# Two transformer blocks in one kernel: query tiles ahead of the gated units, and a first tile in three interleaved passes

## The chip, the cores and the metric

One core of a Trainium2 chip runs the whole program. The metric is the device time of one execution in microseconds (us). TensorE (PE) does the matrix products, VectorE (DVE), ScalarE (ACT) and GpSimd (POOL) do the elementwise work, and SyncE (SP) issues nearly all DMAs. Each engine runs its own instruction list in order and waits on semaphores for the others.

## The reference, cut to what matters

The kernel computes a hybrid layer (sparse attention beside a gated convolution, then cross attention, then a gated feed-forward net) and after it a recurrent layer, for 512 tokens of width 1024. The change lies in the first part of the first layer:

```
h = rmsnorm(x, norm_mix_g);  proj = h @ w_in
q, k, v, qi, ki, wi, glu = split(proj)              # q 512 wide, glu 2*512 wide
q, k, qi, ki = partial_rope(...)                    # tables from the positions
# attention: index scores relu(qi.ki)*wi, top 128 keys per query, 8 heads, 4 query blocks of 128
u  = glu_a * sigmoid(glu_g)
u  = causal_dwconv(u, conv_b_w, conv_b_b)           # 31 taps, 512 channels
b_out = silu(layernorm(u, ln_b_g, ln_b_b))
x  = x + concat(a_out, b_out) @ w_out
kc = m @ w_k_cross;  vc = m @ w_v_cross             # m = rmsnorm(mem), used by the next stage
```

## The kernel before, in words

**Products.** All weights come in chunks of 128 x 1024 fp32 (512 KB). A chunk is split in two reduced-precision parts: ACT casts it to `weights_high` (`high`, L665), POOL subtracts to get `weights_low` (`low`, L588), and activations are split in the same way (`a_high` by ACT, `a_low` by DVE). One block product is three matmuls of 512 columns: high x high, high x low, low x high (L1613). A tile is 8 blocks, 24 matmuls. Raw, high and low weights have two buffers each, so the cast of a chunk waits until the tile two before it is done, and the load two ahead waits for POOL (`load`, L509).

**The first tiles.** `first_tiles` (L1682) does tiles 0 and 1 together: all 16 high x high matmuls as the blocks of `x` land, then the 16 with `a_low`, then the 16 with `weights_low`, and only then is tile 0 done. ACT makes `a_high` and the squares of `x` in turn (L688 to L697). DVE adds up the squares (`add_x`, L1071) between its `a_low` operations, and after that computes the angles of the rope tables (L1091 to L1105).

**The plan.** From there to the end of the first half of the output product every engine walks the same list, `FIRST_PLAN` (L359 to L422), and picks out the items that concern it. That list is the order of the work. Its items: `tile` (a piece of an input tile; its last piece makes ACT cast the next chunk and copy the result out, and POOL make the next `low`), `sum` and `spread` (root mean square of `x`), `key_turn`, `query_turn`, `key`, `query` (rope), `index` (12 index products, relu, weighted sum), `best` (one of 16 rounds of the top-k: three MAX8 and three MATCH_REPLACE8 on DVE), `chosen` (turns the result into a mask), `glu_scale`, `gate`, `glu` (the gated units), `mem_*` (norm of the memory), `fill` (half a chunk of the `kc` or `vc` product), `tap` (a convolution tap on DVE), `product` (a tap made by ACT and added by POOL). Attention is 32 steps (4 query blocks of 8 heads). `logits` of step s, `prob` (transposes) of step s-2 and `value` of step s-3 form one step; a step waits for the mask operation of step s-2 on DVE (L1826). The key width of a step is 128, 256, 384 or 512 by its query block.

Order before: tiles 0 to 3 (index key, index queries, key/value), tile 4 inside the 12 index items, tiles 5 to 11 (with tile 4 the gated units), tiles 12 to 15 (queries). Behind the tiles 5 to 15 stand 15 of the 16 `best` rounds and the first 10 products; then half a fill, the last `best` and `chosen`. Then the 32 steps, with 31 more fills by `FILLS_AT`, 84 taps in steps 0 to 24 and 30 products in steps 0 to 23. `mean` follows step 25, `variance` step 26, `ln_spread` step 28, `ln_low` step 29, and from step 31 the `second` pieces (output product over the convolution half).

Of the kernel before, what the change touches and what calls it, by code (L numbers as in the profile page):

```python
# [7 lines left out]
I32 = mybir.dt.int32  # L8
# [79 lines left out]
def build(nc, w8, w11, xT, memT, mem, positions, params, blockdiag, out):  # L88
    ctx = ExitStack()
    with ctx:  # L90
# [72 lines left out]
        sb("not_early", [P, 4 * (TAPS + 1 + T) + 8 * T + 3 * T + 2 * T], where=s1a)  # L163
        mem_raw = sb("mem_raw", [P, KB, MB * P], where=s1a)
        mem_tok = sb("mem_tok", [P, MB, D], where=s1a)
# [55 lines left out]

        acc = ctx.enter_context(nc.psum_tensor("acc", [P, 2, T], F32))
# [128 lines left out]
        PRODUCTS = [(1, k) for k in range(SHARED_TAPS)] + [(0, k) for k in range(TAPS)]  # L351
        CONV = [(n, k) for n in (2, 3) for k in range(TAPS)] + [(1, k) for k in range(SHARED_TAPS, TAPS)]
        INDEX = [(qb, 2 * half + i) for half in range(2) for qb in range(1, QB) for i in range(2)]

        def adds_before(i):
# [3 lines left out]
        FIRST_PLAN = [("tile", 0, 0, KB), ("tile", 1, 0, KB), ("tile", 2, 0, 4), ("sum",), ("key_turn", 0),  # L359
                      ("spread",), ("wi",), ("query_turn", 0), ("key", 0), ("query", 0), ("tile", 2, 4, KB),  # L360
                      ("mem_scale", 0, 4), ("tile", 3, 0, 4), ("query_turn", 1), ("query", 1),
                      ("tile", 3, 4, KB), ("mem_scale", 4, 8)]
        for n in range(len(INDEX)):
            FIRST_PLAN += [("index", n)] + ([("tile", 4, 2 * (n // 3), 2 * (n // 3) + 2)] if n % 3 == 2 else [])
        FIRST_PLAN += [("causal",), ("glu_scale", 0)]
        BETWEEN = {5: [("key_turn", 1), ("glu_scale", 1), ("mem_high", 0, 4), ("mem_low", 0, 2), ("best",),
                       ("key", 1), ("v",), ("mem_root",)],
                   6: [("glu_scale", 2), ("gate", 0), ("mem_high", 4, 8), ("mem_low", 2, 4), ("best",)],
                   7: [("glu_scale", 3), ("glu", 0), ("best",), ("best",), ("mem_spread",)],
                   8: [("glu_scale", 4), ("gate", 1), ("mem_low", 4, 6), ("best",)],  # L370
                   9: [("glu_scale", 5), ("glu", 1), ("best",), ("mem_low", 6, 8)],
                   10: [("glu_scale", 6), ("gate", 2), ("best",), ("best",), ("product", 0), ("product", 1)],
                   11: [("glu_scale", 7), ("glu", 2), ("best",), ("product", 2)],
                   12: [("gate", 3), ("best",), ("product", 3), ("product", 4)],
                   13: [("glu", 3), ("best",), ("best",), ("query", 2), ("product", 5)],
                   14: [("best",), ("query", 3), ("product", 6), ("product", 7)],
                   15: [("best",), ("best",), ("query", 4), ("product", 8), ("product", 9)]}
        for n in range(5, 16):
            FIRST_PLAN.append(("tile", n, 0, 4))
            if n >= 13:  # L380
                FIRST_PLAN.append(("query_turn", n - 11))
            FIRST_PLAN += [("tile", n, 4, KB)] + BETWEEN[n]
        FILLS = [("fill", n, 4 * half, 4 * half + 4) for n in range(2 * KB) for half in range(2)]
        SECOND = [("second", c, t, 2 * k, 2 * k + 2) for c in range(4) for t in range(2) for k in range(2)]
        FIRST_PLAN += FILLS[:1] + [("query_turn", 5), ("best",), ("query", 5), ("chosen",)]
# [3 lines left out]
        for step in range(len(DSA) + 3):  # L389
            fills = FILLS_AT[step] if step < len(DSA) else 0  # L390
            if step < len(DSA):
                FIRST_PLAN.append(("logits", step))
            FIRST_PLAN += FILLS[:fills // 2 + fills % 2]
            if 2 <= step < len(DSA) + 2:
                FIRST_PLAN.append(("prob", step - 2))
# [15 lines left out]
            if step == 25:  # L411
                FIRST_PLAN.append(("mean",))
# [1753 lines left out]
```

## Time and profile before

| | us |
|---|---|
| median of 3 runs (1431.14 to 1436.74) | 1432.0 |
| the profiled execution | 1433.88 |
| its span | 1432.1 |
| PE busy in the span | 1378.1 (96%) |
| DVE / POOL / ACT busy | 787.3 / 606.6 / 539.4 |
| mean granted clock of PE | 0.981 of full |

The span is what the profile covers; the profiled execution's own time is 1.8 us more. An engine's busy time is the time in which some instruction of it ran. The granted clock is 1.00 at 2.4 GHz and 0.50 at 1.2 GHz. A matmul's duration is modelled and overlaps the next one, so a run of matmuls is better read from the starts.

### The profile page before, as it was taken

The numbers are of one execution on the slowest core, as the hardware profiler recorded it, in microseconds if no ns is written. First come the engines' busy times: TensorE is split into PE (matmuls) and PEld (weight loads), VectorE is DVE, ScalarE is ACT, GpSimd is POOL, SyncE is SP. The second block draws the span as 40 slices with busy tenths as digits, with TensorE's granted clock in tenths as the row PEclk, the third lists the DMA queues.
The fourth block names the chain that finished last, engine by engine and source line by source line (L and its number), as shares of the span: only waits on it lengthen the run. The fifth ranks groups of instructions, "written<-read, shape, count | busy, mean of one in ns | idle before, by whom it ended". The sixth has DMA issues, their size and how long they took to land.

```text
span 1432.1 us, 18114 instructions
## 1 busy us (share of the span) xinstructions
PE 1378.1 (96%) x6240; PEld 1097.8 (77%) x6240; DVE 787.3 (55%) x1077; ACT 539.4 (38%) x843; POOL 606.6 (42%) x295
## 2 busy tenths in 40 slices
PE   7999999999999999999999999999999999999997
PEld 5687766877678888888888777677778888888885
DVE  6698984262366777777633588655463333333232
ACT  4445666343343232332323254434343233233221
POOL 3587971242134444444444443111234444444341
PEclk8999988899999999999999999999999999999999
DMA  6122320122122222222222222111122323233321
GB/s 218 50 91 81 106 72 30 55 85 67 44 74 88 89 101 96 95 103 99 101 101 95 88 74 75 44 45 45 45 76 101 100 90 103 89 107 101 102 87 73
DMA packets 31874, 121.18 MB, mean 85 GB/s; under 512 B 3536, under 2 KB 3664, under 8 KB 31568
## 3 DMA queue, kind: packets, MB, share of 16 engines
q1 hardware_dynamic: 31392, 119.55, 24.7%
q10 hardware_dynamic: 432, 0.96, 0.3%
q8 instruction: 32, 0.52, 0.2%
q14 instruction: 18, 0.15, 0.0%
HBM read 118.40 MB, written 2.10 MB: 84 GB/s over the span
## 4 chain that ended last, share of the span: by engine, by line
PE 75%; issue 13%; POOL 5%; DVE 2%; ACT 2%; DMA 1%; POOLq 0%; SPq 0%; DVEq 0%; ACTq 0%
PE acc L1613 60%; POOL weights_low L588 3%; PE acc L1761 3%; POOL conv L637 2%; PE aux L1983 2%; PE acc L1733 1%; PE aux L1847 1%; PE aux L2003 1%; PE aux L1828 1%; PE aux L1985 1%; PE aux L1836 1%; DMA weights_raw<-w 1%; PE aux L1993 1%; PE aux L1667 0%; PE aux L2019 0%
## 5 line engine op out<-in xcount | busy, mean ns | idle before, releaser
L588 POOL TENSOR_TENSOR weights_low<-weights_raw,weights_high 128x1024 fp32r<-128x1024 f32 (+1 forms) x204 | 525.0, 2574 | 795.9 <-ACT weights_high L665 792.8
L665 ACT CAST weights_high<-weights_raw 128x1024 fp32r<-128x1024 f32 (+1 forms) x202 | 222.1, 1099 | 519.4 <-PE acc L1613 498.2
L1613 PE MATMUL acc<-a_high,weights_high 128*128 128x512 f32 x976 | 389.5, 399 | 5.6 <-POOL weights_low L588 3.0
L1613 PE MATMUL acc<-a_high,weights_low 128*128 128x512 f32 x976 | 381.8, 391 | 0.0
L1613 PE MATMUL acc<-a_low,weights_high 128*128 128x512 f32 x976 | 381.6, 391 | 0.0
L1613 PEld LDWEIGHTS acc<-a_high,weights_high 128*128 128x128 f32 x976 | 184.2, 189 | 49.5 <-issue 7.6
L1613 PEld LDWEIGHTS acc<-a_low,weights_high 128*128 128x128 f32 x976 | 184.2, 189 | 38.9 <-issue 2.1
L1613 PEld LDWEIGHTS acc<-a_high,weights_low 128*128 128x128 f32 x976 | 184.1, 189 | 38.7
L1119 DVE TENSOR_TENSOR residual<-acc,residual 128x512 f32<-128x512 f32 (+1 forms) x56 | 38.5, 688 | 183.2 <-PE acc L1613 145.0
L1613 PE MATMUL acc<-h_high,weights_high 128*128 128x512 f32 x352 | 137.8, 391 | 0.0
L1613 PE MATMUL acc<-h_high,weights_low 128*128 128x512 f32 x352 | 137.2, 390 | 0.0
L1613 PE MATMUL acc<-h_low,weights_high 128*128 128x512 f32 x352 | 137.1, 390 | 0.0
L1298 DVE TENSOR_TENSOR square_sum<-square_sum,square 128x512 f32<-128x512 f32 x44 | 89.1, 2024 | 39.7 <-ACT square L833 19.5
L1390 DVE TENSOR_TENSOR h_low<-work,h_high 128x512 f32 x44 | 86.6, 1969 | 41.6 <-ACT h_high L898 41.6
L1384 DVE TENSOR_TENSOR work<-acc,row_factor 128x512 f32<-128x512 f32 x44 | 30.4, 692 | 105.5 <-PE acc L1613 105.5
L1613 PEld LDWEIGHTS acc<-h_high,weights_low 128*128 128x128 f32 x352 | 66.1, 188 | 13.7
L1613 PEld LDWEIGHTS acc<-h_high,weights_high 128*128 128x128 f32 x352 | 66.1, 188 | 13.5
L1613 PEld LDWEIGHTS acc<-h_low,weights_high 128*128 128x128 f32 x352 | 66.2, 188 | 13.4
L895 ACT ACTIVATE work<-work 128x512 f32<-128x512 f32 x44 | 27.8, 631 | 97.5 <-DVE work L1381 93.9
L1146 DVE SCALAR_TENSOR_TENSOR aux<-glu,par,aux 128x512 f32<-128x512 f32 x78 | 58.8, 754 | 2.0
L1477 DVE TENSOR_TENSOR_SCAN left<-stay 128x128 f32<-128x128 f32 (+3 forms) x32 | 33.6, 1049 | 46.0 <-ACT stay L967 42.9
L1379 DVE SCALAR_TENSOR_TENSOR work<-gated,par,work 128x512 f32<-128x512 f32 x22 | 55.4, 2520 | 3.3 <-DVE work L1377 3.3
(339 smaller groups left out, 1894.0 us busy)
## 6 DMA issues: line engine op xcount, KB each, us to landing
weights_raw<-w SPq DMA_DIRECT2D x172, 512.0 KB, 3.2
weights_raw<-w SPq DMA_DIRECT2D x32, 704.0 KB, 4.0
residual<-xT SPq DMA_DIRECT2D x8, 256.0 KB, 7.2
out<-y_tok SPq DMA_DIRECT2D x4, 512.0 KB, 3.7
mem_raw<-memT SPq DMA_DIRECT2D x1, 1024.0 KB, 5.4
mem_tok<-mem SPq DMA_DIRECT2D x1, 1024.0 KB, 7.5
lru_weights<-blockdiag ACTq DMA_DIRECT2D x1, 512.0 KB, 3.3
sine<-positions ACTq DMA_DIRECT2D x1, 256.0 KB, 6.9
```

The source lines that it names most:

```text
L588: g.tensor_tensor(weights_low[:, s, 0:cols], weights_raw[:, s, 0:cols], weights_high[:, s, 0:cols].bitcast(F32), ALU.subtract).then_inc(we ...
L637: g.tensor_tensor(conv[:, b], conv[:, b], product[:, j % 2], ALU.add).then_inc(last_conv_steps, 1)
L665: a.copy(weights_high[:, s, 0:cols], weights_raw[:, s, 0:cols]).then_inc(weight_high, 1)
L1119: v.tensor_tensor(residual[:, bass.ds(n, 1)].rearrange("p a n -> p (a n)"), acc[:, s], residual[:, bass.ds(n, 1)].rearrange("p a n -> p (a ...
L1146: ins = v.scalar_tensor_tensor(dst, src, weight, sofar, ALU.mult, ALU.add)
L1298: v.tensor_tensor(total_, total_, squares, ALU.add).then_inc(summed, 1)
L1379: own.then(v.scalar_tensor_tensor(work[:, 0], gated[:, 1:1 + T], dcol("fconv_w", c + 1), work[:, 0], ALU.mult, ALU.add))
L1384: v.tensor_tensor(work[:, 1], acc[:, 1], row_factor[:], ALU.mult).then_inc(tile_out[1], 1)
L1390: v.tensor_tensor(at(dst_low, i), work[:, 1], at(dst_high, i).bitcast(F32), ALU.subtract).then_inc(operand_low, 1)
L1477: own.then(v.tensor_tensor_scan(left[:, 0:w][:, ::-1], back, back, 1.0, ALU.mult, ALU.min))
L1613: last = t_.matmul(acc[:, bank, 0:cols], w[:, s, wide], x_[:, k0 + k, 0:cols], start=start and k == opens and n == 0, stop=stop and k == c ...
L1761: last = t_.matmul(acc[:, t], w[:, q % 2, wide], x_[:, block0 + k], start=k == 0 and n == 0, stop=k == 3 and n == 2)
```

## The change

- The columns of `w_in` are ordered so that the queries are tiles 4 to 7 and the gated units tiles 8 to 15.
- Tile 4 begins ahead of the 12 index items; the rest of it and tile 5 stand between them. Tiles 6 and 7, rope, memory norm and four `best` rounds follow, and half of tile 8. The other 15 halves of the gated tiles stand in attention steps 0 to 7, with the other 12 `best` rounds; `chosen` is in step 7.
- The 32 fills stand in steps 8 to 31, at least one in each. The 84 taps are spread over steps 8 to 26, the 40 products over steps 5 to 25. `mean`, `variance`, `ln_spread`, `ln_low` and the start of `second` are each two steps later.
- `first_tiles` does tile 0 in three interleaved passes as blocks of `x` land, tile 1's high x high matmuls between them; tile 0 is then done first, and the 16 other matmuls of tile 1 follow.
- ACT makes all `a_high` first, then two squares, then the cast of chunk 2 (after tile 0), two squares, the copy of tile 0, a square, the cast of chunk 3 (after tile 1), the copy of tile 1, three squares. DVE makes all `a_low`, then the angles with `add_x` between them. The squares have eight tiles of their own (`x_square`), no longer four.
- `positions` is loaded by SP after `x`, no longer by ACT. `mem_root` moves from behind tile 5 to ahead of `sum`.
- Which convolution channels are shared between the engines changes with the order: POOL's are block 0 and the first nine taps of block 3.
- `mem_raw` and `mem_tok` lie elsewhere, so the wait for `mem_low` moves from the first mask to the first taps.

```diff
-        PRODUCTS = [(1, k) for k in range(SHARED_TAPS)] + [(0, k) for k in range(TAPS)]
+        PRODUCTS = ([(0, k) for k in range(16)] + [(3, k) for k in range(SHARED_TAPS)]
+                    + [(0, k) for k in range(16, TAPS)])
...
+        FIRST_PLAN = [("tile", 0, 0, KB), ("tile", 1, 0, KB), ("mem_root",), ("tile", 2, 0, 6), ("sum",),
+                      ("tile", 2, 6, KB), ("key_turn", 0), ("query_turn", 0), ("tile", 3, 0, 2), ("spread",),
+                      ("key", 0), ("query", 0), ("tile", 3, 2, KB), ("query_turn", 1), ("wi",), ("query", 1),
+                      ("mem_scale", 0, 4), ("tile", 4, 0, 4)]
+        IN_INDEX = [("tile", 4, 4, 6), ("tile", 4, 6, KB)] + [("tile", 5, 2 * k, 2 * k + 2) for k in range(4)]
         for n in range(len(INDEX)):
+            FIRST_PLAN += [("index", n)] + (IN_INDEX[n // 2:n // 2 + 1] if n % 2 else [])
+        FIRST_PLAN += [("mem_scale", 4, 8), ("causal",), ("tile", 6, 0, 4), ("key_turn", 1), ("best",),
+                       ("mem_high", 0, 4), ("key", 1), ("tile", 6, 4, KB), ("query_turn", 2), ("v",),
+                       ("mem_low", 0, 4), ("query", 2), ("best",), ("tile", 7, 0, 4), ("query_turn", 3),
+                       ("query", 3), ("mem_high", 4, 8), ("best",), ("mem_spread",), ("tile", 7, 4, KB),
+                       ("query_turn", 4), ("query", 4), ("mem_low", 4, 8)]
+        FILLS = [("tile", n, 4 * half, 4 * half + 4) for n in range(8, 16) for half in range(2)]
+        FILLS += [("fill", n, 4 * half, 4 * half + 4) for n in range(2 * KB) for half in range(2)]
+        FIRST_PLAN += FILLS[:1] + [("query_turn", 5), ("query", 5), ("best",)]
-        FILLS_AT = (1, 1, 2, 1, 2, 1, 2, 1, 1, 1, 2, 1, 1, 1, 2, 1, 1, 1, 1, 0, 1, 1, 1, 0, 1, 0, 1, 0, 1, 0, 1, 0)
-        CONV_STEPS, PRODUCT_STEPS = 25, 24
+        FILLS_AT = (1, 2, 2, 2, 2, 2, 2, 2, 2, 1, 2, 1, 2, 1, 2, 1, 1, 2, 1, 1, 1, 2, 1, 1, 1, 1, 2, 1, 1, 2, 1, 1)
+        BEST_AT = (2, 1, 2, 1, 2, 1, 2, 1)
+        FIRST_TAP, LAST_TAP, FIRST_PRODUCT, LAST_PRODUCT = 8, 26, 5, 25
...
+            if step < len(BEST_AT):
+                FIRST_PLAN += [("best",)] * BEST_AT[step]
+            if step in (4, 8):
+                FIRST_PLAN += [(kind, step // 2 - 2 + i) for kind in ("gate", "glu") for i in range(2)]
+            if step == 7:
+                FIRST_PLAN.append(("chosen",))
+            FIRST_PLAN += [("tap", i) for i in share(len(CONV), step, FIRST_TAP, LAST_TAP)]
+            FIRST_PLAN += [("product", i) for i in share(len(PRODUCTS), step, FIRST_PRODUCT, LAST_PRODUCT)]
...
+            square_x(0)
+            square_x(1)
+            high_next(0, 0)
+            square_x(2)
+            square_x(3)
+            a.copy(kiwi[:], acc[:, 0]).then_inc(tile_out[0], 1)
+            square_x(4)
+            high_next(0, 1)
+            a.copy(qiT[:, 0], acc[:, 1]).then_inc(tile_out[1], 1)
+            for k in range(5, KB):
                 square_x(k)
...
             own.then(v.tensor_scalar(sine[:], cosine[:], col("freq"), None, ALU.mult))
+            add_x(1)
             own.then(v.tensor_scalar(cosine[:], sine[:], float(1 / (2 * np.pi)), ROUND, ALU.mult, ALU.add))
             own.then(v.tensor_scalar(cosine[:], cosine[:], -ROUND, None, ALU.add))
+            add_x(2)
+            own.then(v.scalar_tensor_tensor(sine[:], cosine[:], -TWO_PI[0], sine[:], ALU.mult, ALU.add))
+            add_x(3)
+            own.then(v.scalar_tensor_tensor(sine[:], cosine[:], -TWO_PI[1], sine[:], ALU.mult, ALU.add))
+            add_x(4)
+            own.then(v.scalar_tensor_tensor(sine[:], cosine[:], -TWO_PI[2], sine[:], ALU.mult, ALU.add))
+            add_x(5)
             v.tensor_scalar(sine[:], sine[:], 3.1415925, -3.1415925, ALU.min, ALU.max
                             ).then_inc(angle_ready, 1)
+            add_x(6)
+            add_x(7)
...
+                part(0, 0, 0)
+                part(0, 1, 0)
+                part(0, 0, 2)
+                part(0, 1, 2)
+                part(1, 0, 0)
+                part(1, 1, 0)
+                for k in range(2, KB):
+                    part(0, k, 0)
+                    part(1, k, 0)
+                    part(0, k, 2)
+                    part(0, k - 2, 1)
+                part(0, KB - 2, 1)
+                part(0, KB - 1, 1).then_inc(chunk_done, 1)
                 for k in range(KB):
+                    part(1, k, 1)
+                for k in range(KB):
+                    last = part(1, k, 2)
+                last.then_inc(chunk_done, 1)
```

In `part(s, k, which)` the last argument picks the pass: 0 is high x high, 1 takes `a_low`, 2 takes `weights_low`.

## Rows read from the trace of the kernel before

**Rows 1.** The page: busy us (share of the span) and instructions by engine.

```profile
PE 1378.1 (96%) x6240; PEld 1097.8 (77%) x6240; DVE 787.3 (55%) x1077; ACT 539.4 (38%) x843; POOL 606.6 (42%) x295
```

**Rows 2.** Windows: length, busy by engine (count), granted clock, DMA share, GB/s.

```profile
25.74:28.54 2.80, 0.00 (x0) 0.03 (x1) 2.77 (x2) 1.53 (x2) 2.80 (x2) 1.00 0.00 0
28.54:32.95 4.41, 4.41 (x12) 3.51 (x13) 3.04 (x4) 0.00 (x0) 2.37 (x1) 0.61 0.56 174
61.00:132.07 71.07, 70.80 (x317) 56.16 (x316) 59.10 (x167) 35.55 (x55) 57.80 (x40) 1.00 0.26 86
132.07:218.76 86.69, 79.10 (x437) 61.23 (x435) 78.01 (x152) 55.84 (x121) 71.33 (x44) 0.94 0.26 88
218.89:272.06 53.17, 49.67 (x227) 37.21 (x227) 16.41 (x35) 27.99 (x46) 6.63 (x3) 0.81 0.06 20
```

**Rows 3.** Windows: two stretches at the low clock, and one of part idle at the full.

```profile
230.30:240.50 10.20, 10.20 (x34) 7.19 (x32) 2.11 (x6) 4.18 (x8) 0.00 (x0) 0.52 0.15 51
251.42:262.10 10.68, 10.68 (x39) 8.38 (x39) 0.70 (x2) 5.02 (x10) 2.35 (x1) 0.53 0.14 49
135.00:140.00 5.00, 3.30 (x25) 2.84 (x24) 4.86 (x12) 2.87 (x8) 4.73 (x3) 1.00 0.29 104
```

**Rows 4.** Timeline of PE, first tiles: start, length, instructions [idle before, releaser].

```profile
21.95 3.79 PE L1698 MATMUL acc<-a_high,weights_low 128*128 128x512 f32 x16
32.95 0.95 PE L1776 MATMUL aux<-ones,square_sum 128*128 128x1 f32 x8
```

**Rows 5.** Timeline of DVE and POOL in the first 32 us.

```profile
12.04 2.94 DVE L1083 SCALAR_TENSOR_TENSOR a_low<-residual,par,a_high 128x512 fp32r<-128x512 f32 x2 [1.39 <-ACT a_high L690]
19.96 2.27 DVE L1077 TENSOR_TENSOR square_sum<-square_sum,gate 128x512 f32<-128x512 f32 x3
26.23 2.45 DVE L1098 TENSOR_SCALAR sine<-sine 128x512 f32<-128x512 f32 x1
28.71 2.75 DVE L1101 SCALAR_TENSOR_TENSOR cosine<-sine 128x512 f32<-128x512 f32 x1
11.38 2.38 POOL L588 TENSOR_TENSOR weights_low<-weights_raw,weights_high 128x1024 fp32r<-128x1024 f32 x1 [1.95 <-ACT weights_high L676]
```

**Rows 6.** Waits of DVE from 61 to 219 us: total, times, longest.

```profile
DVE aux L1112 <- PE aux L1795: 6.2, 2, 4.9
DVE masked L1229 <- PE aux L1828: 3.2, 4, 1.8
```

**Rows 7.** Groups by line and form, 132 to 219 us: busy, mean ns.

```profile
L1146 DVE SCALAR_TENSOR_TENSOR aux<-glu,par,aux 128x512 f32<-128x512 f32 x78 | 58.8, 754 | 2.0
L637 POOL TENSOR_TENSOR conv<-conv,product 128x512 f32<-128x512 f32 x30 | 39.0, 1299 | 4.6 <-ACT product L739 2.5
L1229 DVE CUSTOM_DVE_ANT_0 masked<-aux,causal 128x128 f32<-128x128 f32 x8 | 2.3, 284 | 0.0
```

**Rows 8.** Timelines of PE (two steps' first items) and DVE (two rounds' first items).

```profile
182.90 0.91 PE L1828 MATMUL aux<-kT,qT 64*128 64x384 f32 x2
185.94 0.91 PE L1828 MATMUL aux<-kT,qT 64*128 64x384 f32 x2
75.64 1.48 DVE L1199 MAX8 small<-score 128x8 f32<-128x256 f32 x3
78.61 1.47 DVE L1199 MAX8 small<-score 128x8 f32<-128x256 f32 x3
```

**Rows 9.** Timeline of ACT and PE around the layer norm's end.

```profile
241.26 1.11 PE L1667 MATMUL aux<-ident,small 128*128 128x128 f32 x8
251.42 1.97 PE L1847 MATMUL aux<-v_tok,probT 128*128 128x64 f32 x8 [3.50 <-ACT probT L801]
251.99 1.03 ACT L665 CAST weights_high<-weights_raw 128x1024 fp32r<-128x1024 f32 x1
252.92 1.26 ACT L725 ACTIVATE vc<-acc,small 128x512 f32<-128x512 f32 x2
```

More of the change, by code:

```diff
@@ L220, in build @@
         s4.close()
+        x_square = [gate[:, k] for k in range(4)] + [score[:, k] for k in range(3)] + [att_tok[:]]
         acc = ctx.enter_context(nc.psum_tensor("acc", [P, 2, T], F32))
@@ L365, in build @@
[L365 to L377, printed above, removed]
@@ L388, in build, with share @@
-        CONV_STEPS, PRODUCT_STEPS = 25, 24
+        FILLS_AT = (1, 2, 2, 2, 2, 2, 2, 2, 2, 1, 2, 1, 2, 1, 2, 1, 1, 2, 1, 1, 1, 2, 1, 1, 1, 1, 2, 1, 1, 2, 1, 1)
+        BEST_AT = (2, 1, 2, 1, 2, 1, 2, 1)
+        FIRST_TAP, LAST_TAP, FIRST_PRODUCT, LAST_PRODUCT = 8, 26, 5, 25
+        def share(count, step, first, last):
+            steps = last - first + 1
+            at = min(max(step - first, 0), steps)
+            return range(at * count // steps, min(at + (step >= first), steps) * count // steps)
@@ L389, in build @@
         for step in range(len(DSA) + 3):
             fills = FILLS_AT[step] if step < len(DSA) else 0
+            now, FILLS = FILLS[:fills], FILLS[fills:]
             if step < len(DSA):
                 FIRST_PLAN.append(("logits", step))
-            FIRST_PLAN += FILLS[:fills // 2 + fills % 2]
-            if 2 <= step < len(DSA) + 2:
+            for n, item in enumerate(now):
+                if n == (fills + 1) // 2 and 2 <= step < len(DSA) + 2:
+                    FIRST_PLAN.append(("prob", step - 2))
+                FIRST_PLAN.append(item)
+                if item[0] == "tile" and item[3] == KB:
+                    FIRST_PLAN.append(("glu_scale", item[1] - 8))
@@ L395, in build @@
+            if fills < 2 and 2 <= step < len(DSA) + 2:
                 FIRST_PLAN.append(("prob", step - 2))
-            FIRST_PLAN += FILLS[fills // 2 + fills % 2:fills]
-            FILLS = FILLS[fills:]
             if step >= 3:
                 FIRST_PLAN.append(("value", step - 3))
-            if step < CONV_STEPS:
-                FIRST_PLAN += [("tap", i) for i in range(step * len(CONV) // CONV_STEPS,
-                                                         (step + 1) * len(CONV) // CONV_STEPS)]
@@ L743, in _ @@
                 j = n[0] if n else 0
-                if what == "tile" and n[2] == KB:
+                if what == "tile" and n[2] == KB and j >= 2:
                     tile_ends(j)
@@ L1695, in first_tiles, with part @@
-                for s in range(2):
-                    pe.wait_ge(weight_low, s + 1)
-                    for k in range(KB):
-                        last = t_.matmul(acc[:, s], weights_low[:, s, k * P:(k + 1) * P], a_high[:, k],
-                                         start=False, stop=k == KB - 1)
-                    last.then_inc(chunk_done, 1)
+                def part(s, k, which):
+                    w, x_ = ((weights_high, a_high), (weights_high, a_low), (weights_low, a_high))[which]
+                    pe.wait_ge(weight_low if which == 2 else weight_high, s + 1)
+                    if which == 1:
+                        pe.wait_ge(operand_low, OP["x"] + k + 1)
+                    else:
+                        pe.wait_ge(operand_high, OP["x"] + k + 1)
+                    return t_.matmul(acc[:, s], w[:, s, k * P:(k + 1) * P], x_[:, k],
+                                     start=k == 0 and which == 0,
+                                     stop=k == KB - 1 and which == (1, 2)[s])
```

86 lines of the change are left out of this document (25 added, 61 removed).

## The prediction

> **What bounds the kernel now.** I read the page first. PE is busy 96% of the span [rows 1], so only PE's idle time and its slow clock can be won, and everything that the change moves lies before 272 us. I then cut that part into windows [rows 2]. The reader is to see two kinds of loss there. One is idle time: 2.8 us after the first tiles (25.74 to 28.54), 7.6 us in the attention steps beside fills (79.10 busy of 86.69), 3.5 us in the tail (49.67 of 53.17). The other is a granted clock of half speed (1.2 of 2.4 GHz): 0.61 over the 4.4 us behind the first gap, and three stretches of about 10 us each later on, two of which stand in [rows 3] (230 and 251 us; the third, near 193 us, is most of the 0.94 in [rows 2]). A stretch of 10.2 us at half speed costs 5.1 us when PE is what sets the pace.
>
> Next, who sets the pace. From 61.0 to 132.07 us PE is busy 70.80 of 71.07 us: PE sets it, and DVE rests 12.0 us. From there to the last convolution tap at 218.76 us DVE is busy 78.0 (more with the gaps between its instructions) and POOL 71.3 of 86.7 us [rows 2]. There DVE's list of taps (78 of 84 in one group, 0.754 us each [rows 7]) sets the pace, with POOL close behind, and PE waits. From `mean` on PE sets it again. So the change is worth what it does to DVE's position at 132 and 218 us, and to the tail.
>
> **Part 1, first tiles to `sum`.** Before, tile 1 ends at 25.74. Matmuls of 512 columns follow each other by 0.23 us at full clock (16 in 3.79 [rows 4]) and by 0.43 at half. In the new order PE has the same 48 matmuls, the first ten of them at half clock as before; tile 0 needs 24 of them and eight of tile 1, and its last `a_low`. I get tile 0 done at 19.7 and tile 1 at 23.4 us, 2.3 earlier. ACT casts chunk 2 at once and POOL's `low` (2.4 us [rows 5]) ends at 23.3. So the 2.8 us gap in front of tile 2 goes.
>
> But a new one comes at `sum`. Before, the squares were added up by 22.2 us (three adds, 2.27 us, from 19.96 [rows 5]) and `sum` followed tile 2's first half at 32.95 [rows 4]. Now `add_x` 7 is the last of 14 DVE operations behind the last `a_low` (about 18.0), the third add waits for a square that ACT makes only after the cast of chunk 2 (about 21.5), and a DVE operation that reads and writes SBUF stands still while POOL works on its `low`: the clamp takes 2.45 us and the next operation 2.75, and two `a_low` beside a POOL `low` of 2.38 take 2.94, where one alone takes 0.74 [rows 5]. The two `low`s now fall at 21.0 and 24.7, into this very chain. DVE stands at 23.9 after add 2, 25.3 after add 3, 27.6 after the next piece, and then six more operations of 0.5 to 0.7 end at about 31.7. PE is at `sum` at 27.5. It waits 4.5 us. `sum` starts at 32.0 instead of 32.95, with 18 matmuls of tile 2 done instead of 12: 0.95 + 6 x 0.23 = +2.3 us. The gap of 2.8 us was followed by 3.3 us at half speed (0.61 over 4.41 us [rows 2], 1.6 us lost, before `sum`). I take the same loss after the new gap, -1.6; its bounds are 0 and 5.1, what a 10 us stretch costs. A wait for `row_factor` of 0.8 us in PE goes, since `wi` is no longer directly behind `spread`. Front: +1.5, between -2.0 and +7.6 (the upper end if `sum` does not wait: 4.5 and 1.6 more).
>
> **Part 2, index to `chosen`.** Pieces of tiles 4 and 5 are now between the index items (2 tiles, 10.9 us, where 5.45 stood), so DVE ends its index sums at 64.5, not 61.0: -3.5 (it includes the front's +1.5). From there DVE has what it had in the window from 61.0, 59.1 us of work, and eight masks of 0.284 more [rows 2, 7], together 61.4. Its rests shrink: the 12.0 us were mostly waits for query tiles (6.2 us in two waits [rows 6]) that come late; now it rests 2.8 us (for `key_turn` and `v`). A `best` round takes 2.97 us (78.61 less 75.64 [rows 8]), and twelve of them with eight masks are 38 us of DVE beside 15 half tiles and attention items, 46 us of PE: PE is not held up by the masks. `chosen` begins at 64.5 + 61.4 + 2.8 = 128.7 instead of 132.07: **+3.4**. The added wait that I looked at is ACT's: the exponential of step s stands in ACT's list ahead of the cast for the next tile but one, and in step 0 it waits for DVE's four `best` rounds until 91, so the cast and the `low` for tile 10 come some 2 us after PE wants them. That is PE's loss alone; DVE doesn't wait for it. I count 0.6 for the mask of step 8 that then comes late (bounds 0 and 2).
>
> **Part 3, steps 8 to 27.** DVE keeps its 84 taps. Eight 128-wide masks fewer, two 512-wide and one `norm` more cancel. The 3.2 us that DVE waited for PE's logits, mostly in the slow stretch at 193 us [rows 6], go: that stretch began where a step had no fill, and now every step has one. `chosen` (three SBUF operations) now runs beside a busy POOL: -2.0 (bounds 0 and 6, a whole `low` for each). PE has 28 us of work in steps 8 to 15 and 27 in 16 to 23 (a step with one fill is 185.94 less 182.90 = 3.04 us [rows 8]), where DVE has 34 and 34; POOL, 2.4 us per tile and 1.3 per add [rows 5, 7], has 34 and 32. So 86.7 - 3.2 + 2.0 + 0.6 = 86.1, `mean` at 214.8: +0.6.
>
> **Part 4, the tail.** Behind `mean` stand two fills more (2.8 us) and two attention steps' other work less (2 x 2.15): +1.5. The layer norm's operations keep their place to each other. But `value` behind `ln_spread` waits for ACT: before, from `ln_spread`'s end (241.26 + 1.11 [rows 9]) to 251.42, 3.5 us of it idle. Now the last fill's cast (1.03) and the two `vc` copies (1.26 [rows 9]) stand ahead of that copy, and PE has only 4.2 us to do meanwhile: idle 6.8. -3.3. After it I take the same 10 us at half speed as before [rows 3], and the same behind `variance`, whose 32 one-column matmuls and the fp32 items around it stand in the same order.
>
> **Sum.** +3.4 + 0.6 + 1.5 - 3.3 = 2.2 us less. The profiled execution took 1433.88, so 1431.7 for such a one; it stood 1.9 us over the median, so against the median of 1432.0 the forecast is **1430**. A measurement of this kernel tells about 0.5% (7.2 us) from no change, so this is no change.
>
> **Rivals.**
> 1. `sum` does not wait. For it: the `low`s could end just before DVE's operations. Against it: the four lengthened operations in [rows 5]. It gives 4.5 + 1.6 more: 1424.
> 2. The tail is covered. For it: the layer norm chain has one more fill beside it in steps 29 and 30, and half-speed stretches would lengthen PE's work there. Then 6.8 of idle and 5.1 of slow clock go: 1418.
> 3. The clock falls in steps 8 to 23. PE is idle there 13 of 68 us in pieces. In 10.2 us at half speed PE does 5.1 of the 8.3 us of work that DVE's pace asks, so each stretch costs 3.2. Four of them cost 12.8: 1441; with three it is slower by over 0.5%. For it: the share of idle time is higher than before. Against it: 3.30 busy of 5.00 us at 135 kept the clock at 1.00 [rows 3], and every step has a fill. The Trainium skill, TensorE: Matmul & The Clock Gate, section "A second HAM failure mode: psum-queue depth-cycling", says that many small rests between groups of matmuls can make the clock swing to and fro; by that rule this rival would be the forecast, and the row at 135 us speaks against it.
> 4. Casts behind exponentials. If each of the six later half-tile pairs of steps 1 to 7 waits 2 us as tile 10 does, PE and then DVE lose 12: 1442. Against it: by my times DVE's masks are ahead from step 2 on.
>
> **Chances.** Forecast 0.50 (its own range 1425 to 1436), rival 1 0.16, rival 2 0.09, rival 3 0.15, rival 4 0.10. Faster 0.28 (rivals 1 and 2 and a little of the forecast), same 0.50, slower 0.22. Range 1419 to 1441: it leaves out the far side of rivals 2 to 4.
>
> **What would show it.** No idle time before tile 2, but 4 to 5 us before `sum`, released by the adds of squares. `chosen` near 129 us. PE idle in pieces under 2 us from step 8 on at clock 1.00. `mean` near 215. An idle of 6 to 7 us before a `value` in the tail, released by ACT's copy. The forecast fails if `sum` comes before 29 us, if the clock reads 0.5 anywhere between steps 8 and 26, or if the tail from `mean` to the last heads is under 48 us.

## The result

The changed kernel takes 1441.8 us (median of 4 runs, 1441.3 to 1442.4) against 1432.1 us: a ratio of 1.0069 (95% interval 1.0052 to 1.0086), 7 to 12 us slower. The forecast was 1430 us and no change. In the profiled executions the span grows by 7.4 us, from 1432.1 to 1439.5. Each window below comes from one profiled execution; where that execution lies far from the median of its kernel, the text says so. The page of the changed kernel:

```profile
span 1439.5 us, 18150 instructions
...
PE 1380.6 (96%) x6240; PEld 1096.8 (76%) x6240; DVE 791.5 (55%) x1077; ACT 542.4 (38%) x845; POOL 607.0 (42%) x295
```

The engines do the same work as before [rows 1]. What has changed is when PE rests and at which clock it runs. I cut the front into the same parts in both traces, by the start of one instruction each:

| start of | before, us | after, us | part got longer by |
|---|---|---|---|
| `sum` | 32.95 | 29.20 | -3.8 |
| `chosen` | 132.07 | 132.21 | +3.9 |
| `mean` | 218.89 | 229.04 | +10.0 |
| end of the span | 1432.1 | 1439.5 | -2.7 |

The windows of the changed kernel follow (columns as in [rows 2]): first the stretch behind `sum`; then the eight steps with the half tiles; then steps 8 to 27, which answer to the row of 132.07 to 218.76; three stretches inside them; and the tail as far as the last `heads`, which answers to the last row of [rows 2].

```profile
29.30:42.80 13.50, 13.50 (x33) 8.31 (x34) 0.85 (x5) 4.32 (x6) 2.35 (x1) 0.52 0.12 39
...
86.02:132.21 46.19, 45.07 (x201) 35.57 (x201) 43.96 (x139) 21.02 (x43) 27.91 (x19) 1.00 0.24 80
132.21:229.04 96.83, 86.85 (x468) 67.92 (x467) 81.08 (x144) 64.16 (x122) 86.09 (x56) 0.89 0.23 77
152.00:158.40 6.40, 6.34 (x26) 5.37 (x27) 2.65 (x4) 4.38 (x10) 6.26 (x5) 0.51 0.26 83
185.50:195.70 10.20, 9.23 (x28) 6.28 (x27) 9.88 (x18) 5.95 (x12) 8.49 (x6) 0.50 0.26 97
219.60:222.90 3.30, 3.30 (x12) 2.67 (x11) 3.16 (x6) 2.15 (x5) 3.16 (x3) 0.52 0.32 99
229.04:276.23 47.19, 40.39 (x192) 30.68 (x191) 12.62 (x25) 24.36 (x37) 7.08 (x3) 0.82 0.13 44
```

The reader is to look at two things: POOL's work (the fifth engine), which is 86.09 us of 96.83 where it was 71.33 of 86.69, and the granted clock, the number after the five engines. From 132 to 229 us it is 0.89, where it was 0.94. Three stretches of 6.4, 10.2 and 3.3 us ran at half speed; in the same steps before there was one. While PE is at half speed DVE falls short too: 2.65 us busy of 6.40 in the first. So the loss is not only PE's: DVE's taps stand behind the masks, and these wait for PE.

What PE did just before each fall, from PE's timeline (start, length, instruction, idle time before it and what ended that):

```profile
29.20 1.87 PE L1803 MATMUL aux<-ones,square_sum 128*128 128x1 f32 x8 [4.39 <-DVE square_sum L1088]
...
152.06 1.12 PE L1874 MATMUL aux<-v_tok,probT 128*128 128x64 f32 x4 [2.92 <-ACT probT L812]
...
184.90 0.47 PE L1760 MATMUL acc<-weights_high,m_high 128*128 128x512 f32 x1 [1.57 <-DVE kcT L1234]
...
219.21 0.47 PE L1760 MATMUL acc<-weights_high,m_high 128*128 128x512 f32 x1 [2.76 <-ACT vc L735]
...
264.57 1.97 PE L1874 MATMUL aux<-v_tok,probT 128*128 128x64 f32 x8 [6.80 <-ACT probT L812]
```

Each of the five has half speed right behind it (the last one 0.50 over its next 3.0 us). I follow the second of them back, since it has no counterpart before. ACT and POOL of the changed kernel from 144 us on:

```profile
144.67 2.15 POOL L637 TENSOR_TENSOR glu<-glu,gate 128x512 f32<-128x512 f32 x2
...
146.78 5.55 POOL L643 TENSOR_TENSOR conv<-conv,product 128x512 f32<-128x512 f32 x4
...
148.16 0.72 ACT L750 ACTIVATE product<-glu,par 128x512 f32<-128x512 f32 x1 [2.49 <-POOL conv L643]
...
149.59 0.72 ACT L750 ACTIVATE product<-glu,par 128x512 f32<-128x512 f32 x1 [0.71 <-POOL conv L643]
...
150.22 0.49 ACT L804 ACTIVATE prob<-masked,small 128x256 f32<-128x256 f32 x1
...
150.71 1.03 ACT L670 CAST weights_high<-weights_raw 128x1024 fp32r<-128x1024 f32 x1
151.64 0.36 ACT L812 COPY probT<-aux 128x256 f32<-128x256 f32 x1
```

Read it from the top. In step 8 POOL has the last two gated units, and the adds of the convolution come behind them, four in a row. `product` has two buffers, so ACT waits 2.49 and then 0.71 us for an add to free one. The exponential (`prob`), a cast of 1.03 us and the copy of `probT` stand behind those products in ACT's list. The copy ends at 152.0, and PE, which wanted it at 149.1, starts at 152.06. Over the whole stretch ACT's two large waits are these (total, times, longest). In the kernel before they were 22.2 and 7.0 us: ACT waits less for DVE now and more for POOL.

```profile
ACT prob L804 <- DVE small L1243: 12.3, 10, 2.3
ACT product L750 <- POOL conv L643: 11.2, 11, 2.5
```

### The profile page after: what moved, and what is told of

Its sections match the earlier page's. It is cut to its first block, busy times and chain, and to the rows that moved or that the text cites. A ratio compares the mean times of both kernels' runs of the same rounds, so it can differ in the third digit from the quotient of the medians.

```text
span 1439.5 us, 18150 instructions
## 1 busy us (share of the span) xinstructions
PE 1380.6 (96%) x6240; PEld 1096.8 (76%) x6240; DVE 791.5 (55%) x1077; ACT 542.4 (38%) x845; POOL 607.0 (42%) x295
## 4 chain that ended last, share of the span: by engine, by line
PE 72%; issue 13%; POOL 6%; DVE 5%; ACT 2%; DMA 0%; POOLq 0%; SPq 0%; DVEq 0%; ACTq 0%
PE acc L1627 60%; POOL weights_low L594 3%; POOL conv L643 3%; PE acc L1788 3%; PE aux L2010 2%; PE aux L2030 1%; PE acc L1760 1%; PE aux L2012 1%; PE aux L1874 1%; PE aux L2020 1%; PE aux L1681 0%; DVE square_sum L1088 0%; PE aux L2046 0%; PE aux L1855 0%; DVE a_low L1316 0%
## 5 line engine op out<-in xcount | busy, mean ns | idle before, releaser
L1627 PEld LDWEIGHTS acc<-h_high,weights_high 128*128 128x128 f32 x352 | 66.1, 188 | 13.5
L906 ACT ACTIVATE work<-work 128x512 f32<-128x512 f32 x44 | 27.8, 631 | 97.5 <-DVE work L1395 93.9
```

The lines of the kernel that those rows point to most:

```text
L1627: last = t_.matmul(acc[:, bank, 0:cols], w[:, s, wide], x_[:, k0 + k, 0:cols], start=start and k == opens and n == 0, stop=stop and k == c ...
```

## The experiments

All are compared with the kernel before in runs on the same chip. C stands for the theory that PE's rests let its clock fall, and that half speed, where PE can no longer keep the pace, is what costs.

**Which half of the change costs.** `old_front` puts the old first stage into the changed kernel; `old_plan` puts the new first stage into the kernel before.

```
old_front: first_tiles, square_x, add_x and the load of positions as before; plan new
old_plan:  first_tiles, square_x, add_x and the load of positions new; plan as before
```

> The new plan with the first tiles, squares, adds and the positions load of the kernel before. Theory A (the loss is in the plan, steps 8 to 27, where POOL's adds and ACT's order hold up the rest; the new first stage gains and loses about the same): the index items of the new kernel begin at 51.2 us, before's at the same point at 51.0, so this stays near the changed kernel, 1439 to 1443. Rival B (the wait of 4.4 us ahead of `sum` and the 13 us at half speed behind it are what the change costs): this comes back to 1432 to 1435.

> The plan of the kernel before with the new first tiles, squares, adds and positions load. Theory A: within 4 us of the kernel before, 1430 to 1436, with a wait of some 6 us ahead of `sum`. Rival B: most of the loss is here, 1438 to 1442.

Measured: `old_front` 1442.2 us, ratio 1.0063 (1.0044 to 1.0081), 97.0 us from `chosen` to `mean`. `old_plan` 1434.4 us, 1.0017 (1.0003 to 1.0031), 82.5 us for the same part of it. The loss is in the plan: the new plan is slow with either front. The first stage's own gain does not arrive either: in `old_plan`, too, PE waits before `sum` and then runs at half speed.

```profile
30.25 1.87 PE L1798 MATMUL aux<-ones,square_sum 128*128 128x1 f32 x8 [5.35 <-DVE square_sum L1083]
```

```profile
30.25:43.30 13.05, 12.26 (x31) 7.96 (x32) 6.14 (x13) 2.79 (x4) 0.00 (x0) 0.50 0.00 0
```

`old_plan` also gives the price of one stretch at half speed. The kernel before and `old_plan` walk the same list from `chosen` to `mean`, and both have PE wait 1.9 us at the same item. Only in the kernel before does half speed follow, near 193 us. The wait before, the same wait in `old_plan`, and the window of `old_plan`:

```profile
191.81 0.47 PE L1733 MATMUL acc<-weights_high,m_high 128*128 128x512 f32 x1 [1.92 <-ACT vc L725]
```

```profile
195.44 0.47 PE L1755 MATMUL acc<-weights_high,m_high 128*128 128x512 f32 x1 [1.93 <-ACT vc L731]
```

```profile
135.72:218.22 82.50, 74.68 (x436) 58.26 (x435) 77.73 (x152) 55.51 (x121) 71.39 (x44) 1.00 0.27 92
```

It is 86.82 us with PE busy 79.23 in the one, 82.50 with 74.68 in the other: one stretch cost 4.3 us there (one execution of each).

**The wait at `sum`.**

```diff
-("tile", 2, 0, 6), ("sum",), ("tile", 2, 6, KB), ("key_turn", 0), ("query_turn", 0),
+("tile", 2, 0, KB), ("key_turn", 0), ("query_turn", 0), ("sum",),
```

> The changed kernel with `sum` moved behind the rest of tile 2, `key_turn` and `query_turn`, 4.1 us of PE work later, so that the adds are ready. Both theories: no wait ahead of `sum`, no stretch at half speed behind it. If the front is on the path: `chosen` ends about 6 to 10 us earlier and the time is 1431 to 1436. Rival: from the index items on DVE's own list decides or the gain turns into waits in steps 8 to 27, and the time stays over 1438.

Measured: 1435.6 us, 1.0020 (1.0002 to 1.0039). The wait falls from 4.4 to 2.0 us but does not go, and half speed still follows it, for some 6 us instead of 13.5. `chosen` comes at 126.9 instead of 132.2. The median is 6.2 us below the changed kernel's; the profiled execution, at 1440.5, was one of the slowest of its ten. From `chosen` to `mean` it takes 98.8 us, so that loss stays when the front's shrinks.

**Which list holds steps 8 to 27.** `thin_adds` does POOL's 38 adds there on 8 columns of 512, `thin_taps` 78 of DVE's 84 taps on 8 columns, `thin_both` both; these leave out that part of the convolution.

```diff
-g.tensor_tensor(conv[:, b], conv[:, b], product[:, j % 2], ALU.add)
+g.tensor_tensor(conv[:, b, 0:8], conv[:, b, 0:8], product[:, j % 2, 0:8], ALU.add)
-v.scalar_tensor_tensor(dst, src, weight, sofar, ALU.mult, ALU.add)
+v.scalar_tensor_tensor(dst[:, 0:m], src[:, 0:m], weight, sofar[:, 0:m], ALU.mult, ALU.add)
```

> The changed kernel with POOL's 38 convolution adds on 8 of 512 columns (the rest of these sums is left out): the same waits, but some 1.1 us of POOL less for each. Theory A (POOL's adds hold ACT's products, these hold the copies and casts behind them in ACT's order, PE waits and its clock falls): the 97 us from `chosen` to `mean` shrink to 82 to 87, no half-speed stretch there, and the time is 1427 to 1432. Rival C (DVE's taps and the idle pieces of PE alone set that pace and drop the clock): 1438 to 1442.

> The changed kernel with 78 of DVE's 84 convolution taps on 8 of 512 columns (the rest of these sums is left out): some 47 us of DVE less, every wait kept. The run with thin adds moved the time by only 2.4 us, so POOL's adds alone don't set the pace. Theory C (DVE's list sets it): the stretch from `chosen` to `mean` falls from 97 to below 88 us and the time to 1430 or below, where POOL's 86 us of work in it begins to hold. Rival D (the waits among PE, ACT and DVE over short fills and banks, with the clock's falls, set it, whoever is busy): over 92 us, 1436 to 1440.

> Adds and taps both thin (both sums left out but for 8 columns). Theory C: only PE is left in steps 8 to 27, some 75 us of work there: the stretch is 75 to 80 us, no wait of PE of over 1 us, no half-speed stretch before `variance`, time 1418 to 1424. Rival D: it stays over 85 us and the clock still falls there.

Measured: 1439.5 us (1.0051, 1.0030 to 1.0072), 1439.9 us (1.0052, 1.0034 to 1.0069) and 1423.7 us (0.9942, 0.9927 to 0.9957). Their windows from `chosen` to `mean`, in that order; then ACT's longest waits in the first and in the second:

```profile
129.86:225.71 95.85, 86.78 (x469) 68.02 (x467) 80.00 (x144) 63.42 (x122) 45.22 (x56) 0.89 0.23 78
133.36:227.40 94.04, 84.55 (x468) 66.25 (x467) 41.07 (x144) 63.37 (x122) 85.69 (x56) 0.93 0.23 79
133.06:211.85 78.79, 77.45 (x468) 61.55 (x467) 40.56 (x144) 63.11 (x122) 45.40 (x56) 1.00 0.27 94
```

```profile
ACT prob L804 <- DVE small L1243: 20.6, 14, 2.3
```

```profile
ACT product L750 <- POOL conv L643: 20.7, 17, 2.8
```

Halving one engine's work gives little: 1.0 and 2.8 us in this part, in profiled executions that took 1444.2 and 1442.3, and 2.4 and 1.9 us in the medians. ACT serves both lists: with POOL light, all its waiting moves to DVE's masks; with DVE light, to POOL's adds. Either way PE's operands come late. Only without both does PE run through, 77.45 us of matmuls in 78.79 at the full clock. This row also splits the time, on PE's side. Of the 18.0 us between 96.83 and 78.79, PE's added idle time is 9.98 - 1.34 = 8.6 us, and its added busy time, the same work at a lower clock, is 86.85 - 77.45 = 9.4 us. That is a split of time and not of causes: `thin_both` takes the waits and the slow clock away together, so it does not show which of them costs the time.

**Order inside a step, and the tail.** `heads_first` puts the step's products behind its `heads`; `ln_early` puts `ln_spread` and `ln_low` at steps 29 and 30 instead of 30 and 31; `norm_mid` puts `norm` behind a step's second tap.

```diff
-FIRST_PLAN += [("product", i) ...]                       # heads_first: now behind ("heads_out", ...)
-if step == 30:  ("ln_spread",) ... if step == 31: ("ln_low",)
+if step == 29:  ("ln_spread",) ... if step == 30: ("ln_low",)
-FIRST_PLAN += [("tap", i) ...]; [("product", i) ...]; ("norm", ...)
+FIRST_PLAN += taps[:2]; ("norm", ...); taps[2:]; [("product", i) ...]
```

> The changed kernel with the `product` items of a step behind `heads` and `heads_out`: in ACT's list the cast of the turned heads then stands ahead of the products that wait for POOL. In steps 11, 19 and 27 DVE waits 4.2 us and less for that cast. If this wait is on the path: 3 to 6 us faster than the changed kernel, 1436 to 1439. If DVE's rest there is made good later: 1440 to 1442.

> The changed kernel with `ln_spread` and `ln_low` one step earlier (29 and 30), so that one more step with a fill stands between ACT's layer norm block and the end of the fills. If the 6.8 us wait of PE for the copy of step 29 comes from too little PE work beside ACT's block: it falls to 3 to 4 us and the time by 3 to 8 us (with what the clock gives back), 1434 to 1439. Rival (the block is only moved and waits for `variance` instead): no change, 1440 to 1443.

> norm stands between a step's second and third tap instead of behind all its taps and products. In the changed kernel the half-speed stretches at 152.0 and 185.5 follow PE waits of 2.92 and 1.57 us around norm's att_tok. Theory L (a lump of waiting at norm starts each fall): the waits shrink by the two or three taps now behind norm (about 1.5 us each), one or two of the three stretches go, and 3 to 8 us are won: 1434 to 1439. Rival E (DVE's denser taps and POOL's additional adds set the pace; the place of the wait does not matter): the rests come elsewhere, chosen to mean stays 94 to 98 us, and the time 1440 to 1442.

Measured: 1441.7 us (1.0070, 1.0048 to 1.0092), 1439.9 us (1.0052, 1.0034 to 1.0070), 1440.4 us (1.0062, 1.0041 to 1.0082). None of these intervals is clear of the changed kernel's own. In `heads_first`, DVE's wait of 4.2 us for the cast falls to 0.7, but its wait for PE at `kcT` grows from 2.6 to 6.0 in sum, so the rest has only moved. In `ln_early`, the 6.8 us wait in the tail becomes two of 2.06 and 1.74. In `norm_mid` the part from `chosen` to `mean` took 93.9 us in the profiled execution, but the wait before the first fall is still there, released by ACT's `probT` and not by `norm`. The theory that `norm` makes the lump fails for that place:

```profile
151.73 1.11 PE L1876 MATMUL aux<-v_tok,probT 128*128 128x64 f32 x4 [2.88 <-ACT probT L814]
```

**Work that keeps PE busy.** The added matmuls' results are read by nobody.

```diff
+if 6 <= j < 25:
+    t_.matmul(turn_bank(what, j)[:, 0:256], rotate[:], qT[:, 0, 0:256], start=True, stop=True)
 pe.wait_ge(prob_raw, j + 1)
```

> 19 matmuls of 256 columns whose results nobody reads stand ahead of the wait for prob in steps 8 to 26: some 0.37 us each (0.590 us for 512 columns of the same kind), 7 us of work added to PE. Theory C (the clock is what costs: PE rests between items, its clock falls, and at half speed it can no longer keep DVE's pace): PE's full-speed work there was 77.5 us with both lists thin, now about 84.5, still under DVE's and POOL's 86; if the added work keeps the clock at 1.00 the stretch from chosen to mean falls from 96.8 to 87 to 90 us and the time to 1433 to 1436. Rival W (PE is simply too full there and the half speed is a by-product): the stretch grows by most of the 7 us, to 100 to 104, and the time to 1445 to 1449.

Measured: 1442.5 us, 1.0071 (1.0050 to 1.0092). The window answers to the one of 96.83 us:

```profile
132.22:230.90 98.68, 91.16 (x507) 72.79 (x506) 81.53 (x144) 63.94 (x122) 86.03 (x56) 0.93 0.23 76
```

Neither number came. The clock did rise, from 0.89 to 0.93, but the work put in is some 7 us by the estimate on record, and PE is busy 4.3 us longer. The part grew by 1.9 us, less than was put in and more than C allows. So padding did not pay here, and C, that the clock alone costs the time, is not confirmed: with part of the clock won back the part was no shorter.

**The burst and the length of POOL's list.**

```diff
-[("product", i) for i in share(len(PRODUCTS), step, 5, 25)]
+[("product", i) for i in share(12, step, 5, 7)]            # prod_early
+[("product", 12 + i) for i in share(len(PRODUCTS) - 12, step, 8, 25)]
+[("product", i) for i in share(6, step, 5, 7)]             # prod_skip
+[("product", 6 + i) for i in share(len(PRODUCTS) - 6, step, 10, 25)]
```

> 12 of the 40 products (and their adds on POOL, about 1.3 us each) stand in steps 5 to 7 instead of 5, the other 28 in steps 8 to 25: some 7 adds or 9 us of POOL's work leave the stretch behind chosen, which was 86 us of POOL's work in 96.8 us. Theory P (POOL's additional adds and the burst behind the gated units hold ACT at product, prob stands behind it, PE waits for probT and its clock falls): ACT's waits for POOL's conv (11.2 us) fall below 5, the PE wait of 2.9 us at probT goes, chosen to mean 88 to 92 us, and the time 1434 to 1438. Rival D (DVE's taps in 19 steps instead of 25 hold prob by themselves, as with thin adds): the PE wait moves to DVE's att_tok, chosen to mean 94 to 97, and the time 1439 to 1442.

> 6 products in steps 5 to 7 and none in steps 8 and 9, where POOL has the gated units' last products and a low; the other 34 in steps 10 to 25, so POOL's list behind chosen keeps its length. If the burst alone starts the first fall of the clock (theory P's burst): the 2.9 us wait for probT and the half-speed stretch of 6.4 us behind it go, 4 to 6 us are won in that place, but the adds are denser later, which gives some back: chosen to mean 91 to 95, the time 1436 to 1440. If the length of POOL's list is what counts: 96 to 99 us and 1441 to 1444.

Measured: 1444.8 us (1.0077, 1.0057 to 1.0097; six runs from 1438.7 to 1448.9) and 1442.6 us (1.0076, 1.0054 to 1.0098; 1437.5 to 1447.4). First the window of `prod_early` from `chosen` to `mean`; behind it that of `prod_skip`, and a stretch in it where the changed kernel had its first half speed:

```profile
128.70:228.30 99.60, 85.37 (x468) 66.99 (x467) 82.80 (x144) 62.30 (x122) 83.61 (x54) 0.90 0.23 75
```

```profile
130.80:223.90 93.10, 83.23 (x469) 64.68 (x468) 81.59 (x144) 63.27 (x121) 84.85 (x55) 0.95 0.24 80
143.00:155.00 12.00, 9.51 (x70) 8.44 (x70) 11.28 (x23) 6.98 (x15) 10.66 (x8) 1.00 0.27 88
```

`prod_early` failed as an experiment. Only three of the 38 adds left the part behind `chosen`, and one `low` came into it (54 POOL operations against 56), because POOL works in order and the adds queued behind the gated units. Its profiled execution was the slowest of six; in it PE waited 2.85 us for a `low` at 139.1 and 3.39 us for `probT` at 144.4, so the burst did harm earlier. `prod_skip` did in its profile what theory P's burst said: the 2.9 us wait for `probT` is gone, 143 to 155 us ran at the full clock, and the part took 93.1 us. But that execution was the fastest of its six, and the median is no better. So the burst stands behind that one wait in the trace; it is not shown to be what the kernel pays for.

**Towards a better version.** `all_four` is the changed kernel with `norm_mid`, `heads_first`, `ln_early`, and `sum` behind the first quarter of tile 3. `five` adds the early products to it. `old_plan_sum` is the old plan with the new first stage, `sum` at that later place and the first rope items behind the whole of tile 2.

```diff
-("tile", 2, 0, 6), ("sum",), ("tile", 2, 6, KB), ("key_turn", 0), ("query_turn", 0), ("tile", 3, 0, 2), ("spread",),
+("tile", 2, 0, KB), ("key_turn", 0), ("query_turn", 0), ("tile", 3, 0, 2), ("sum",), ("tile", 3, 2, 4), ("spread",),
```

> The changed kernel with four edits together: sum behind tile 3's first piece, norm between the taps, the products behind heads, ln_spread and ln_low one step earlier. If the gains add (sum later alone gave 6.2 us, the layer norm earlier 1.9, the products 0.2, norm by theory L 3 to 8): 1426 to 1431. If theory E holds and the middle stretch stays at 95 us or more: 1432 to 1436, no better than the kernel before.

> The old plan behind the new first stage, with sum behind the first piece of tile 3. That plan with sum at its old place took 1434.4, with a wait of 5.3 us at sum and the clock at half speed for about 13 us behind it. Theory C: without the wait both go, 5.3 + 6.5 us less up to sum, of which DVE's list from 132 us on keeps some: 1424 to 1429, faster than the kernel before. Rival (DVE's list of index sums and best rounds, not PE, sets when chosen comes, so the front's gain is absorbed): 1431 to 1434.

> The four edits together with the 12 early products. With theory P the gain of prod_early (4 to 8 us) adds to the four edits' time of 1427.7: 1420 to 1424. With rival D: 1426 to 1429, no different.

Measured: `all_four` 1427.7 us (0.9970, 0.9955 to 0.9985; 12 runs), `old_plan_sum` 1428.9 us (0.9979, 0.9962 to 0.9996; 12 runs), `five` 1431.5 us (0.9989, 0.9977 to 1.0001). The first two are faster than the kernel before by 4.4 and 3.2 us, and so faster than the changed one. `five` came at neither of its two numbers: with the early products its part from `chosen` to `mean` took 98.6 us. In `all_four`, PE's start of `sum`, and then the window behind it and the one from `chosen` to `mean`:

```profile
31.31 1.05 PE L1805 MATMUL aux<-ones,square_sum 128*128 128x1 f32 x8 [0.26 <-DVE square_sum L1090]
```

```profile
31.30:41.70 10.40, 10.29 (x54) 8.14 (x54) 7.64 (x16) 4.33 (x6) 2.54 (x2) 1.00 0.16 50
122.71:218.80 96.09, 84.64 (x469) 66.58 (x468) 81.05 (x144) 62.67 (x120) 85.90 (x56) 0.93 0.24 78
```

`chosen` comes 9.5 us earlier than in the changed kernel, with next to no wait at `sum` and without half speed behind it. The part from there to `mean` still takes 96.1 us, though its clock is 0.93 and not 0.89, so in these two executions nearly all of the gain is the front's (that of `all_four`, at 1430.5, was the slowest of its twelve). `old_plan_sum` keeps the old plan's short part (84.0 us) but reaches `chosen` only at 128.6: DVE's rope holds the index there, and half speed follows. So the two end almost level by opposite ways: in `all_four` `chosen` comes 5.9 us earlier, `mean` 6.2 later, and the rest is 5.3 us shorter. With `sum` moved, and with its three other edits, the new plan is no slower than the old one.

```profile
41.48 1.96 PE L1839 MATMUL aux<-kiT,qiT 64*128 64x256 f32 x6 [2.87 <-DVE qiT L1123]
```

## Why the prediction was wrong

**Part 1, first tiles to `sum`: the wait right, its price wrong.** Tile 2 starts without a gap, at 20.47 us (forecast 23.4: no half clock among the first matmuls in this execution). The wait before `sum` is 4.39 us, forecast 4.5, by the chain that was named. Both its ends came 2.6 us early, PE at 24.8 instead of 27.5 and the adds at 29.1 instead of 31.7; in the execution of `thin_adds`, whose first matmuls did run at half clock, `sum` came at 31.4 behind 4.03 us. DVE and POOL in the changed kernel:

```profile
18.03 2.58 DVE L1102 TENSOR_SCALAR cosine<-cosine 128x512 f32<-128x512 f32 x1
...
21.97 2.78 DVE L1088 TENSOR_TENSOR square_sum<-square_sum,gate 128x512 f32<-128x512 f32 x1
```

```profile
17.91 2.42 POOL L594 TENSOR_TENSOR weights_low<-weights_raw,weights_high 128x1024 fp32r<-128x1024 f32 x1 [5.70 <-ACT weights_high L670]
21.58 2.63 POOL L594 TENSOR_TENSOR weights_low<-weights_raw,weights_high 128x1024 fp32r<-128x1024 f32 x1 [1.25 <-ACT weights_high L670]
```

Two DVE operations that take 0.43 and 0.69 us alone take 2.58 and 2.78, and end 0.3 and 0.5 us behind POOL's `low`. The Trainium skill (GPSIMD Engine Reference, "1. Specifications") says that the two engines share their SBUF interfaces, with contention for DVE instructions in a 2-port mode or with two SBUF inputs. The add has two SBUF inputs, and its row agrees; the other has one, and the trace does not show its mode. The half-speed stretch behind the wait was priced at 1.6 us by its forerunner, with 5.1 as the upper bound. It lasted 13.5 us at 0.52 and cost 6.5. `all_four`, with a wait of 0.26 us left, ran this stretch at 1.00.

**Part 2, index to `chosen`: right in the main.** Forecast 128.7, measured 132.2. Of the 3.5 us, 2.1 were there when the index sums ended (66.6, forecast 64.5): Part 1's clock term was 4.9 short, and `sum` came 2.8 earlier than its 32.0. The other 1.4 us arose behind it and I have not traced them. `chosen` took 2.75 us beside POOL, forecast 2 us more than before, and 86 to 132 us ran at 1.00 with PE 45.07 busy of 46.19, so rival 4 (casts behind exponentials, 12 us) did not happen.

**Part 3, steps 8 to 27: the step that failed.** It forecast 86.1 us at the full clock: DVE's list sets the pace, POOL's is "close behind", and the clock costs nothing, since rests come "in pieces under 2 us" and every step has a fill. It took 96.8 us at a clock of 0.89. Two terms of it were wrong.

The first is the pace. POOL's list in this part has 86.09 us of work, up from 71.33 [rows 2]: 8 adds more and the last gated units. A part of 86.1 us would have left POOL no rest at all. The thin runs show that DVE's and POOL's lists hold the part up together, and that neither alone does.

The second is the clock term, put at nothing. PE is busy 86.85 us with matmuls that take 77.45 at the full clock, and this 9.4 us is most of the 10.7 missing. It is rival 3, held at 0.15. Its event came, and its price was too low: 3.2 us for 10.2 us at half speed, where the one stretch that `old_plan` lacks cost 4.3. It took PE to need 8.3 us of work in 10.2; the thin run shows 77.45 in the 86.1 that DVE's pace allows, 9.2 in 10.2. At that pace the three stretches, 19.9 us, ask for 17.9 us of work where PE at half speed does at most 10.0. (Its 1441 is also a slip: 1430 and 12.8 make 1442.8.) But how much of the 9.4 us the clock cost here stays open. Where it fell less, PE rested more: in `ln_early` it read 0.93 in this part, PE was busy 84.0 us, and the part still took 96.3.

The argument against rival 3 rested on a misread row. The 3.30 busy of 5.00 us at 135 us [rows 3] are not many small rests; they are one rest of 1.70 us, in this line of the kernel before:

```profile
137.35 0.36 PE L1613 MATMUL acc<-m_high,weights_high 128*128 128x256 f32 x1 [1.70 <-POOL weights_low L588]
```

So no row spoke against small rests. Nor does the length of a single wait decide. In the changed kernel half speed stood behind waits of 2.92, 1.57 and 2.76 us; waits of 1.70 here, of 1.93 in `old_plan` and of 2.04 in `prod_skip` had none behind them, and neither had the very wait of 1.57 us at `kcT` in `sum_late`, where 180.0 to 183.9 us read 1.00:

```profile
180.02 0.47 PE L1760 MATMUL acc<-weights_high,m_high 128*128 128x512 f32 x1 [1.58 <-DVE kcT L1234]
```

How POOL's adds hold up ACT, and ACT PE, is followed in the rows above for the wait at 152 us alone. The Trainium skill (TensorE: Matmul & The Clock Gate, "A second HAM failure mode: psum-queue depth-cycling") says that frequent small rests between groups of matmuls can make the clock swing; by that rule rival 3 was the forecast. The result is on its side in that the clock did swing; whether the small rests or the three long ones did it, no run here tells.

**Part 4, the tail.** The wait of 6.8 us was forecast to the tenth (6.80, released by ACT's `probT`). But the tail is not 1.8 us longer in sum; by the table it gives 2.7 back. PE is busy 40.39 of 47.19 us at 0.82 where it was 49.67 of 53.17 at 0.81. At the full clock that is some 8 us less work, of which about 3 are two pieces of the next phase that now stand later; the forecast knew of some 1 to 2 of the rest. The other 3 to 4 us I have not traced. Half speed behind `variance`, forecast as before, came again (240 to 246 us, 0.50 to 0.55), and PE had not rested in front of it.

By the prediction's own tests: `sum` came at 29.2, just after the 29 us that would have failed it; the clock did read 0.5 between steps 8 and 26; and the tail was 47.2 us, under the 48 named.

**What stays open.** Why the clock falls behind a wait in one execution and not behind the same wait in another. `prod_early` and `prod_skip` spread over 10 us between runs, the changed kernel's four over 1. Nor is it shown whether the waits or the slow clock cost the time in steps 8 to 27, as no run of the new plan took away the one and kept the other; only `old_plan` did so, for one stretch of the old plan. No single wait, taken away, brought the part from `chosen` to `mean` below 93 us. Keeping the taps in 25 steps inside the new plan would test the packing by itself; it was not tried, since the gated units are not ready earlier there.

## What to carry to other kernels

Where a matmul engine is 90% full, a wait can cost twice: itself, and a half-speed stretch behind it (4.3 us for one in the old plan, 6.5 us for the one behind `sum`). Before packing side work more densely, add up the lists of all engines over the same steps, and not the longest one alone. Here they were 77, 81 and 86 us, the part took 97, and thinning one list gained 1 to 3 us where thinning two gained 18. And move a small item that waits for a chain of adds behind independent matmuls: in the changed kernel the shorter move of `sum_late` turned 1441.8 us into 1435.6, and in the old plan a longer one, with the first rope items moved too, 1434.4 into 1428.9.

## What the runs showed of the hardware that I had not expected

- Half speed behind a wait of PE lasted from 3.3 to 13.5 us (windows above), and followed waits as short as 1.57 us. It does not follow each: a wait of 2.04 us in `prod_skip` had none behind it; the window of 143 to 155 us around it, above, reads 1.00:

```profile
149.78 0.63 PE L1875 MATMUL aux<-v_tok,probT 128*128 128x64 f32 x4 [2.04 <-DVE att_tok L1255]
```
- Half speed also came without any wait. In `old_plan` it set in right after the one-column matmuls of `variance` and lasted for 30 us, in which PE never rested:

```profile
228.00:258.00 30.00, 30.00 (x94) 20.30 (x94) 8.56 (x19) 18.02 (x29) 3.61 (x2) 0.51 0.05 18
```
- The wait of 4.4 us before `sum` cost another 6.5 us by the clock, 10.9 in all. Moving `sum` and `spread` behind other matmuls won 9.5 of them at `chosen`.
- The first matmuls of tiles 0 and 1, at half clock in the profile of before, were at 1.00 in that of after, and tile 2 began 2.9 us before the forecast's time. That is not the new order alone: of the 15 profiled executions with the new first tiles, 8 read 1.00 from 7 to 15 us and 7 did not, `thin_adds` among them (0.50 from 11 to 15 us).
